# Two buffers for the merged rows, first value tiles loaded in the fronts, accumulators loaded late, normalisation in two operations

## The reference

```python
merged = sigmoid(gate_a) * (attn @ w_br_attn) + sigmoid(gate_b) * (rwkv_out @ w_br_rwkv)
h = layer_norm(ALPHA * x + merged @ w_out, ln1_g, ln1_b)
y = layer_norm(ALPHA * h + peer(h, peer_q, peer_keys, peer_u, peer_v), ln2_g, ln2_b)

def one_block(xb):                       # peer, for 128 rows
    q = (xb @ peer_q).reshape(128, 8, 2, 64)
    s = einsum("bhcd,hckd->bhck", q, peer_keys)          # 8 heads, 2 halves, 128 keys
    sv, si = top_k(s, 16)
    cand = sv[:, :, 0, :, None] + sv[:, :, 1, None, :]   # 256 candidates a head
    fv, fi = top_k(cand, 16)                             # 16 experts a head, of 16384
    gate = softmax(fv)
    act = gelu(einsum("bhkd,bd->bhk", peer_u[eidx], xb))
    return einsum("bhk,bhkd->bd", gate * act, peer_v[eidx])
```

## Time and profile before

| | us |
|---|---|
| median of 3 runs | 4496.24 (4477.59 to 4502.65) |
| the profiled execution | 4525.03 |
| its span | 4523.2 |
| early front | about 685 to 829 |
| late front | about 2547 to 3056 |
| dense stage | about 3056 to 4523 |

### The profile page before, as it was taken

How to read it: one execution, slowest core, us unless ns; L and a number is a source line. 1 busy time by engine, 2 the same in 40 slices (tenths; PEclk the granted TensorE clock), 3 DMA queues, 4 the chain that set the end, 5 groups by cost and what they waited for, 6 DMA issues and landing times. The chain is left out here.

```text
span 4523.2 us, 71734 instructions
## 1 busy us (share of the span) xinstructions
PE 3806.4 (84%) x28122; PEld 2543.4 (56%) x28122; DVE 3106.4 (69%) x6050; ACT 874.0 (19%) x1788; POOL 1830.6 (40%) x1489
## 2 busy tenths in 40 slices
PE   7977888899979688887877786667999999999997
PEld 6766665655545487876654364553544445444543
DVE  0455422578778567775967478885889888967778
ACT  1332220110222122322531012560000000000000
POOL 0016000056212133332336207834666666666774
PEclk9988888899999898987878887678999999999998
DMA  7552443399889657675559633439999999999997
GB/s 171 168 154 89 134 153 129 119 341 410 197 202 214 186 193 254 218 237 174 174 202 404 260 136 47 94 105 353 407 403 395 394 403 407 389 401 407 404 400 281
DMA packets 438548, 1154.59 MB, mean 255 GB/s; under 512 B 84497, under 2 KB 179260, under 8 KB 434588
## 3 DMA queue, kind: packets, MB, share of 16 engines
q0 software_dynamic: 207216, 687.87, 43.3%
q1 hardware_dynamic: 194564, 422.08, 27.1%
q10 hardware_dynamic: 36432, 40.05, 2.6%
HBM read 1045.72 MB, written 114.70 MB: 257 GB/s over the span
## 5 line engine op out<-in xcount | busy, mean ns | idle before, releaser
L2677 PE MATMUL x_sps<-c_big,l_c_wo 128*128 128x384 f32 x2048 | 691.8, 501 | 93.3 <-DMA l_c_wo<-u_cols 82.9
L381 POOL DMA_INDIRECT l_w_ring<-u_rows,k_eidx x256 | 300.8, 1175 | 973.7 <-DVE l_w_dots L437 443.8
L2684 PE MATMUL x_vps<-x_v,x_w 128*128 128x512 f32 x1536 | 662.3, 592 | 2.1 <-DVE x_w L2717 2.1
L381 POOL DMA_INDIRECT w_ring<-u_rows,k_eidx x384 | 482.7, 1257 | 442.9 <-DVE w_dots L437 276.3
L2677 PEld LDWEIGHTS x_sps<-c_big,l_c_wo 128*128 128x128 f32 x2048 | 400.4, 196 | 385.1 <-DMA l_c_wo<-u_cols 90.4
L454 DVE SCALAR_TENSOR_TENSOR w_yacc<-w_ring,w_wts,w_yacc 128x1024 f32<-128x1024 f32 x384 | 493.4, 1285 | 64.4 <-DMA w_ring<-v_rows,k_eidx 52.9
L2684 PEld LDWEIGHTS x_vps<-x_v,x_w 128*128 128x128 f32 x1536 | 291.7, 190 | 366.7 <-issue 357.8
L437 DVE CUSTOM_DVE_ANT_0 w_ring<-w_ring,w_h 128x1024 f32<-128x1024 f32 x384 | 452.2, 1223 | 55.2 <-DMA w_ring<-u_rows,k_eidx 28.3
L381 POOL DMA_INDIRECT w_ring<-v_rows,k_eidx x384 | 429.8, 1119 | 133.3 <-issue 113.4
L381 POOL DMA_INDIRECT l_w_ring<-v_rows,k_eidx x256 | 283.6, 1108 | 345.5 <-DVE l_w_yacc L454 283.6
L454 DVE SCALAR_TENSOR_TENSOR l_w_yacc<-l_w_ring,l_w_wts,l_w_yacc 128x1024 f32<-128x1024 f32 x256 | 329.0, 1285 | 51.4 <-DMA l_w_ring<-v_rows,k_eidx 43.0
(11 more groups left out here) (643 smaller groups left out, 6171.0 us busy)
## 6 DMA issues: line engine op xcount, KB each, us to landing
l_c_wo<-u_cols SPq DMA_DIRECT2D x128, 512.0 KB, 7.2
x_v<-v_rows SPq DMA_DIRECT2D x128, 512.0 KB, 12.2
e_c_w<-w_tiles SPq DMA_DIRECT2D x54, 512.0 KB, 3.7
l_c_w<-w_tiles SPq DMA_DIRECT2D x54, 512.0 KB, 7.4
l_c_wo<-s_G SPq DMA_DIRECT2D x16, 1536.0 KB, 23.1
s_rw<-l_q_out SPq DMA_DIRECT2D x48, 384.0 KB, 12.9
s_G<-l_f_stage ACTq DMA_DIRECT2D x8, 2048.0 KB, 8.0
s_zT<-l_pz ACTq DMA_DIRECT2D x30, 384.0 KB
```

Of the source, the lines that this page charges most:

```text
L381: pool.indirect_dma_start(out=self.ring[:, r, :], out_offset=None, in_=self.A[table], in_offset=bass.IndirectOffsetOnAxis(ap=idx[:, s:s + ...
L2677: mm = pe.matmul(sps[n % 2][:, 0:ND * P], u[n % 4][:, k, :], hT[:, k, :], start=(k == 0), stop=(k == KT - 1))
L2684: mm = pe.matmul(vps[k][:, x * 512:(x + 1) * 512], w[:, e, k * P:(k + 1) * P], v[:, e, x * 512:(x + 1) * 512], start=(c == 0 and e == 0), ...
```

## The change

- `fronts` has two buffers `mTb` with a semaphore each. `load(0)` and `load(1)` come first on SP, ahead of the decode rows' small loads, `iota`, `ln`, `wq` and `keys`; `load(i)` waits for `mix(i - 2)`.
- `wq` has no tile of its own: it lies in a tile `sb_v` of the same size, allocated around the front. In the late part this tile outlives the front and is the dense stage's v. Behind the last query of the front SP loads the first chunk's v tiles into it (`last_q`, `v_ahead`), and the front's end waits for them.
- The dense stage doesn't load v for chunk 0, and loads `acc` behind `load_v` of chunk 14 (at c = 13).
- ACT's order for i = 2: the copies of the scores come before `soften(0)`.
- In `norm`, `scaled` and `token_scaled`, (x - mean) * rs, times ln gain, plus ln offset (three operations) become ((x - mean) * gain) and (times rs + offset): two `scalar_tensor_tensor`.

```diff
-        lnk(V.tensor_scalar(x, x, ag[:, 0:1], rs, ALU.subtract, ALU.mult))
-        lnk(V.tensor_tensor(x, x, self.ln[0:rows, 0, :], ALU.mult))
-        self.mark(dve, V.tensor_tensor(x, x, self.ln[0:rows, 1, :], ALU.add), done_s, n)
+        lnk(V.scalar_tensor_tensor(x, x, ag[:, 0:1], self.ln[0:rows, 0, :], ALU.subtract, ALU.mult))
+        self.mark(dve, V.scalar_tensor_tensor(x, x, rs, self.ln[0:rows, 1, :], ALU.mult, ALU.add), done_s, n)
...
-        wq = sb("f_wq", [P, KT, DM])
+        wq = A["sb_v"]
...
-        mTb = sb("f_mTb", [P, KT, P])
+        mTb = [sb(f"f_mTb{j}", [P, KT, P]) for j in range(2)]
...
-                if i:
-                    sp.wait_ge(S["mixed"], i)
+                if i >= 2:
+                    sp.wait_ge(S["mixed"], i - 1)
...
+            load(0)
+            load(1)
             if dec_rows:
...
-            load(0)
...
-            load(1)
             n_ahead = ahead(sp, S["ahead_in"])
...
             n_ahead += last(sp, S["ahead_in"])
+            sp.wait_ge(S["q_psum"], NF)
+            n_ahead += last_q(sp, S["ahead_in"])
...
                 query(i)
+                for c in range(2):
+                    scores(i, c)
                 if picks and i == 2:
                     soften(0)
-                for c in range(2):
-                    scores(i, c)
...
             load_g(0)
             rows.begin(sp)
-            load_v(0)
-            for k, b in enumerate(DENSE):
-                sp.dma_start(acc[:, k, :], A["h"][b]).then_inc(S["acc_in"], 16)
...
                 if c + 1 < NCH:
                     load_v(c + 1)
+                if c == NCH - 3:
+                    for k, b in enumerate(DENSE):
+                        sp.dma_start(acc[:, k, :], A["h"][b]).then_inc(S["acc_in"], 16)
...
-                        pe.wait_ge(v_in[e], 16 * (c + 1))
+                        if c:
+                            pe.wait_ge(v_in[e], 16 * c)
...
+    def v_ahead(sp, sem):
+        for e in range(CH):
+            sp.dma_start(A["sb_v"][:, e, :], A["v_rows"][e * NKEY:(e + 1) * NKEY]).then_inc(sem, 16)
+        return CH
```

More of the change, by code:

```diff
@@ L2059, in finish, with fronts @@
         do(dve, "b3", V.tensor_tensor(to, to, self.gate[:, :, :], ALU.mult))
-def fronts(nc, A, tag, blocks, picks, strewn, scat, ahead, last, few=False, dec_rows=False):
+def fronts(nc, A, tag, blocks, picks, strewn, scat, ahead, last, last_q, few=False, dec_rows=False):
     NF, NST, NSC, NPK = len(blocks), len(strewn), len(scat), len(picks)
@@ L2104, in fronts @@
         gps = [psum(f"f_gps{j}", 512) for j in range(2)]
-        names = ("const_in iota_in ln_in m_in mixed h0_done var_done std_done h_done hT_psum hT_done q_psum q_done sc_psum "
+        m_in = [sem(f"f_m_in{j}") for j in range(2)]
+        names = ("const_in iota_in ln_in mixed h0_done var_done std_done h_done hT_psum hT_done q_psum q_done sc_psum "
                  "sc_done sc_out ahead_in sc_in scs_read fv_done fe_done idx_done idx_psum byslot_done one_done two_done g_psum g_done link "
@@ L2129, in load @@
             def load(i):
-                if i:
-                    sp.wait_ge(S["mixed"], i)
-                sp.dma_start(mTb[:, :, :], A["mT"][:, :, blocks[i] * P:(blocks[i] + 1) * P].rearrange("t p c -> p t c")).then_inc(S["m_in"], 16)
+                if i >= 2:
+                    sp.wait_ge(S["mixed"], i - 1)
+                sp.dma_start(mTb[i % 2][:, :, :], A["mT"][:, :, blocks[i] * P:(blocks[i] + 1) * P].rearrange("t p c -> p t c")).then_inc(m_in[i % 2], 16)
                 if i >= 2:
@@ L2202, in mix @@
                 if c == 0:
-                    pe.wait_ge(S["m_in"], 16 * i + 16)
+                    pe.wait_ge(m_in[i % 2], 16 * (i // 2) + 16)
                     if i:
@@ L2206, in mix @@
                 for k in range(KT):
-                    mm = pe.matmul(fps[:, c * 512:(c + 1) * 512], mTb[:, k, :], wo[:, k, c * 512:(c + 1) * 512],
+                    mm = pe.matmul(fps[:, c * 512:(c + 1) * 512], mTb[i % 2][:, k, :], wo[:, k, c * 512:(c + 1) * 512],
                                    start=(k == 0), stop=(k == KT - 1))
@@ L2451, in norm @@
                 lnk(V.reciprocal(rs[:, :], rs[:, :]))
-                lnk(V.tensor_scalar(hi[:, :], hi[:, :], ag[:, 0:1], rs[:, 0:1], ALU.subtract, ALU.mult))
                 if i == 0:
                     dve.wait_ge(S["ln_in"], 16)
-                lnk(V.tensor_tensor(hi[:, :], hi[:, :], ln[:, 0, :], ALU.mult))
-                mark(V.tensor_tensor(hi[:, :], hi[:, :], ln[:, 1, :], ALU.add), S["h_done"], i + 1)
+                lnk(V.scalar_tensor_tensor(hi[:, :], hi[:, :], ag[:, 0:1], ln[:, 0, :], ALU.subtract, ALU.mult))
+                mark(V.scalar_tensor_tensor(hi[:, :], hi[:, :], rs[:, 0:1], ln[:, 1, :], ALU.mult, ALU.add), S["h_done"], i + 1)
             def choose(k, x):
@@ L2531, in token_scaled @@
                 lnk(V.reciprocal(d_rs[0:NS, :], d_rs[0:NS, :]))
-                lnk(V.tensor_scalar(d_y, d_y, d_ag[0:NS, 0:1], d_rs[0:NS, :], ALU.subtract, ALU.mult))
-                lnk(V.tensor_tensor(d_y, d_y, d_ln[:, 0, :], ALU.mult))
-                mark(V.tensor_tensor(d_y, d_y, d_ln[:, 1, :], ALU.add), S["d_done"], 1)
+                lnk(V.scalar_tensor_tensor(d_y, d_y, d_ag[0:NS, 0:1], d_ln[:, 0, :], ALU.subtract, ALU.mult))
+                mark(V.scalar_tensor_tensor(d_y, d_y, d_rs[0:NS, :], d_ln[:, 1, :], ALU.mult, ALU.add), S["d_done"], 1)
             norm(0)
@@ L2599, in experts @@
         u = A["sb_u"]
-        v = sb("x_v", [P, CH, DM])
+        v = A["sb_v"]
         w = sb("x_w", [P, CH, ND * P])
@@ L2627, in load_v @@
             def load_v(c):
-                if c:
-                    sp.wait_ge(S["v_psum"], ND * c)
+                sp.wait_ge(S["v_psum"], ND * c)
                 for e in range(CH):
@@ L2792, in program @@
             trunk(PARTS[0], none, nothing, c4)
-            fronts(nc, A, "e_", [NB] + EARLY, [], [], [], x_ahead, none_ahead, few=True)
+            A["sb_v"] = c4.enter_context(nc.sbuf_tensor("e_c_v", [P, CH, DM], F32))
+            fronts(nc, A, "e_", [NB] + EARLY, [], [], [], x_ahead, none_ahead, none_ahead, few=True)
         with ExitStack() as c4:
@@ L2799, in program @@
             A["sb_hT"] = wide(ND * P)
+            A["sb_v"] = c4.enter_context(nc.sbuf_tensor("l_c_v", [P, CH, DM], F32))
+            assert CH == KT
             A["sb_u"] = [A["sb_wo"][:, j, :].rearrange("p (k n) -> p k n", k=KT) for j in range(4)]
-            fronts(nc, A, "l_", [b for b in range(NB) if b not in EARLY], DENSE + FETCHED_2[:1], STREWN, [b for b in DENSE if b not in STREWN], none_ahead, u_ahead, dec_rows=True)
+            fronts(nc, A, "l_", [b for b in range(NB) if b not in EARLY], DENSE + FETCHED_2[:1], STREWN, [b for b in DENSE if b not in STREWN], none_ahead, u_ahead, v_ahead, dec_rows=True)
             experts(nc, A)
```

## The result

| us | before | changed |
|---|---|---|
| median of 7 runs each, side by side | 4486.56 (4475.94 to 4502.65) | 4439.06 (4429.24 to 4456.68) |
| the profiled execution | 4525.03 | 4429.24 |
| its span | 4523.2 | 4427.4 |

The ratio is 0.9897, with a 95% interval from 0.9877 to 0.9916: 1.0% faster, 46.2 us of 4486.56, with an interval from 37.7 to 55.2 us (the two medians are 47.5 apart). The forecast was 4448, a ratio of 0.9893 and 48.3 us. The interval is wide: the forecast's 48.3 and the 39.7 of the rival "the fronts give less" both lie in it, and the 37.3 of "only the bytes count" is just outside. Which of them holds has to come from the stages.

What follows compares the result with a forecast made beforehand. PE's matmuls, u loads, and DVE with the gathers were taken to share the dense stage, the fronts not living on transfers. Terms -5.2, -13.8, -1.4, -3.5, -25.6, +4, -2.8 sum to -48.3: ratio 0.9893, 4448.3 us; range 4427 to 4478.

Steps and rivals of the forecast that it cites:

- the fronts give less: Rival, both fronts: the clock falls in the 1.5 us gap too (5.6) and wq is late (3); -39.7, 4457; chance 0.12.
- only the bytes count: Rival, dense stage: it gains only v's 4.2 MB, 10.6 us instead of 25.6 - 4; total -37.3, 4459; chance 0.2.
- ACT's order: Late front, i = 2: decode sums come earlier, so DVE's 1.36 us wait for them goes; -1.4 us.
- dense: chunk 0: Stall for the fifth u tile falls from 29.88 to 7 us (bounds 0 and 15); chunk 92.1 instead of 117.7, -25.6.
- acc +4: Chunk 14: acc's three loads, 1.6 MB, stand ahead of its fifth u tile; +4 us, from 0 to +8.
- Mixes and clock: Both fronts: gap before the second mix falls to 1.5 us, and the mix takes 14.00; early -5.2, late -13.8.
- the margin of 2 us: Late front: wq in before about 2581, wanted by PE at 2583.4; its later load costs nothing, or up to 3 us.
- Normalisation: Two operations for three, -0.7 us each: five on the late front's path (3.5), four at the end (2.8).
- v in the front: End of the late front: chunk 0's v lands by about 3030 to 3035, before the last store at 3047.05; cost 0.
- The mean of the others should stay at 88.1: Dense stage: chunks other than the first keep their mean of 88.1 us; a rise would mean bytes or lost lead.
- DVE loses its lead: Rival, dense stage: without the long stall gathers and v compete, 92.4 us a chunk; in all +12, 4508; chance 0.06.
- order: Dense stage: PE's chunk 0 stall comes from loads queued ahead of the fifth u tile; reordering wins it, 25.6 less 4.

Runs made afterwards that it cites:

- f1: The kernel before with only the two `mTb` buffers and the new order of the fronts' first loads; 4521.68 us, ratio 0.9954 to the kernel before.
- g2: The changed kernel with each front's second mix waiting for the first block's whole normalisation; fronts 144.0 and 490.2 us, against 137.6 and 485.4.
- n0: The changed kernel with the three-operation normalisation put back in all three places; 4503.22 us, one run.
- a1: The changed kernel with acc loaded behind the last u tile of chunk 15; 4486.64 us, ratio 0.9898 to the kernel before, dense stage 1439.3 us.
- a3: The same kernel as a1, run again beside the changed kernel on one chip; 4436.66 us, ratio 0.9894 to the kernel before, dense stage 1442.7 us.
- d1: The kernel before with chunk 0's v issued behind its u tiles and acc at c = 13, no byte leaving the stage; 4530.51 us, ratio 0.9987.

## Why the prediction was right, point by point

| us | forecast | by the stages |
|---|---|---|
| early front | -5.2 | -6.3 |
| late front: mixes, ACT's order, norms | -18.7 | -18.5 |
| dense: chunk 0 | -25.6 | -30.1 |
| dense: from chunk 1 to the end (acc +4, norms -2.8) | +1.2 | +9.3 |
| sum | -48.3 | -45.6 |

The chunk 0 row is the mean of 117.7 and 116.0 (f1) against 86.8, the mean of the five traces; the row under it 1350.7 against 1360.0.

*Mixes and clock.* Both steps came as written: gap 1.4 for 1.5, 13.97 for 14.0. That the 2.8 of the clock hangs on PE's idling is seen in g2, where it partly returned, and in the granted clock; its size at a given gap is not what I assumed (below). The row that the 14.00 was taken from was a favourable one: in the kernel before, the next two mixes of the late front took 16.71 and 16.54 without idling directly ahead of them. PE's wait ahead of the first transposes is 0.32, for the keys: wq and keys came just in time, so the margin of 2 us was used up but the term of 0 held. POOL's gathers start 5.5 us behind the first mix instead of 2.5 ahead of it and were covered. DVE's first choice in the kernel before, then DVE and POOL of the changed kernel:

```profile
2639.14 0.29 DVE L165 MAX8 k_sv<-k_scs 128x8 f32<-128x128 f32 x1 [14.27 <-DMA k_scs<-s_sc]
```

```profile
2567.54 0.29 DVE L165 MAX8 k_sv<-k_scs 128x8 f32<-128x128 f32 x1 [14.20 <-DMA k_scs<-s_sc]
...
2664.67 1.27 DVE L2520 SCALAR_TENSOR_TENSOR c_big<-c_big,l_f_gps 8x512 f32<-8x512 f32 x2
```

```profile
2500.20 0.93 POOL L2308 DMA_INDIRECT l_f_stage<-u_rows,k_didx  x1 [41.36 <-DMA k_dgate<-s_d_gate]
```

The choice comes 72.88 us behind the first mix (2567.54 less 2494.66) instead of 86.63 (2639.14 less 2552.51 in the earlier trace rows): 13.75 sooner, for 13.8. That it fits to 0.05 is partly luck. PE's part, to the end of the first block's scores, is 72.5 before and 60.8 changed, 11.7 sooner: the first mix (16.53 for 15.40) and the query (17.43 for 16.19) took longer. The other 2.1 are the scores' store and fetch, 12.0 for 14.1, which the forecast had not counted.

*ACT's order.* The decode sums at 2664.67 have no wait any more (1.36 in the earlier trace rows); undone, a wait of 2.17 was back and the front behind the first choice was 1.6 longer, for 1.4. One run.

*Normalisation.* -2.8 for -3.5 in the front (one run of n0) and -2.6 for -2.8 at the end (the same in every trace), together 5.4 for 6.3.

*v in the front.* Cost 0, as said. From ACT's last store to the first `x_sps` it is 9.34 us in both kernels (2970.68 to 2980.02; 3047.05 to 3056.39 in the earlier trace rows), though the eight loads were issued from 2937.51 on. ACT and SP of the changed kernel:

```profile
2970.68 0.37 ACTq L2382 DMA_DIRECT2D s_G<-l_f_stage  x1
```

```profile
2935.71 1.76 SPq L2753 DMA_DIRECT2D l_c_wo<-u_cols  x4
2937.51 5.05 SPq L2758 DMA_DIRECT2D l_c_v<-v_rows  x8
```

*Chunk 0, mis-sized.* The stall left over was put at 7 us, with bounds 0 and 15; it was 1.96. Half of the rate for SP beside the gathers was nearly right: by it the fifth tile comes 26.4 us after the stage's start, and it came after 25.0, which by the forecast's own working is a stall of 2.1. What failed is the step from the 3.5 us of that working to "7 us for this stall and the slower start after it, like the longest of the other chunks": no slower start followed.

*The rest of the stage, the step that failed.* "The mean of the others should stay at 88.1" did not hold. From chunk 1 to the end the stage is 9.3 longer. Of this a1 and a3 show 5.4 to be acc (1354.6 against 1360.0; forecast 4), and the norms take off 2.6, so 6.5 is left that the forecast had at 0. Chunk 1 alone is 9.6 longer. It is the mechanism of the rival that DVE loses its lead, at its place but in one chunk instead of fourteen. (That rival's "worst" chunk, 92.4, was not the worst: chunk 9 of the kernel before took 93.1, by which its sum would have been +22 instead of +12.) POOL at the start of chunk 1, first the kernel before and then the changed one, and DVE of the changed one:

```profile
3173.56 0.94 POOL L381 DMA_INDIRECT w_ring<-u_rows,k_eidx  x1 [0.30 <-issue]
3187.63 1.14 POOL L381 DMA_INDIRECT w_ring<-u_rows,k_eidx  x1 [13.13 <-DVE w_dots L437]
```

```profile
3071.62 0.93 POOL L381 DMA_INDIRECT w_ring<-u_rows,k_eidx  x1 [0.30 <-issue]
3080.56 1.14 POOL L381 DMA_INDIRECT w_ring<-u_rows,k_eidx  x1 [8.01 <-DVE w_dots L437]
```

```profile
3072.99 0.56 DVE L2717 TENSOR_TENSOR x_w<-x_w,l_c_wo 128x384 f32<-128x384 f32 x1 [1.89 <-ACT x_w L2694]
```

The first 20 us of chunk 1 as windows (columns as above), of the kernel before and of the changed one:

```profile
3174.07:3194.07 20.00, 20.00 (x64) 11.78 (x63) 9.40 (x14) 1.57 (x4) 5.67 (x5) 1.00 1.03 410
```

```profile
3067.00:3087.00 20.00, 20.00 (x63) 11.78 (x62) 13.29 (x24) 1.57 (x4) 9.58 (x9) 1.00 1.03 410
```

Before, the ring was full and POOL stood still for 13.13 us; with five gathers in these 20 us, more of the same 410 GB/s was SP's. Changed, the pause is 8.01, POOL has nine gathers in these 20 us, DVE's idle time falls from 7.01 to 1.89, and the fifth u tile comes 6.71 late. Later chunks alternate between 82 to 85 and about 91 to 92 as they did before. The place is read from the traces, and d1 (91.8 in chunk 1) shows that removing the stall alone brings it about.

How far the gathers were ahead can be counted: gathers that POOL has started, less the tiles that DVE has begun to multiply or add. At the start of chunk 1 it is 10, all the buffers, in the two traces with the long stall (before and f1: chunk 1 82.5), and 7 or 8 in the twelve others (87.7 to 92.8). The same holds further on. In chunks 1 to 13 of all fourteen traces, the 25 chunks that started with 10 tiles ahead took 82.5 to 84.9, mean 83.3; the 78 that started with 7 or fewer had a mean of 91.0 and none was below 84.8; 8 and 9 lie between (89.0 and 85.4). So the lead goes with the chunk's length wherever one looks, and one or two long chunks rebuild it (in the changed kernel it was 7, 10, 7 at chunks 1, 2, 3, which took 92.4, 82.6 and 92.4). It remains an association: no run set the lead by itself.

*Between "order" and "bytes".* The rival "only the bytes count" said 4459 and the forecast 4448: in reductions 37.3 and 48.3, with 46.2 by the timing. The sum was right, what it was credited to was not. In d1, with the order but not the bytes, the stage gave 4.6 of the 21.6 that the forecast had for order alone (25.6 less 4). The changed kernel's dense stage is 16.2 shorter than d1's (1463.0 less 1446.8); the norms are 2.6 of that, so 13.6 are left for the 4.2 MB of v that leave the stage, 10.6 at the full rate. Nearly all of it lies in chunk 0 (98.6 against 86.8), where in d1 DVE stood for gathered rows while v was on the way; from chunk 1 on d1 took 1364.3 and the changed kernel, with the norms put back, 1362.6. Of the 20.8 of the stage, the bytes are thus the larger part (13.6) and the order the smaller (4.6). This is a difference between one trace and the mean of five. The Trainium skill's statement (DMA: Bandwidth & Descriptors, Issuing engines are not separate DMA queues) that transfers of all issuing engines run on the same 16 engines and interleave agrees with d1, where DVE waited 6.75 us for rows that POOL had asked for while SP's loads of v ran.

So the total was right in part by luck, with two errors that partly cancel: 4.5 too little for chunk 0 (and 1.1 for the early front), and 8.1 too much credit behind it.

## What to carry to other kernels

Where the DMA engines are full, a long stall of the matmul engine is no measure of what removing it gives: ask first which bytes leave the stage, and look at the chunk behind the stall for what the stall had been giving to others. Loads moved into a stage whose engines have room (v in the front) gained their whole transfer here (13.6 us for 4.2 MB), and a load that nobody awaits (acc) belongs behind the last one that somebody does. Compare traces by the stage that is touched, and for a small term by a stretch between two of its own events: untouched stages here varied by more than the whole effect, the late front by 3 us, and the stretch from the last gathered add to the end by less than 0.1.

## What the hardware showed that I had not expected

- After an idle gap PE's 32 matmuls took 13.97 us (gap 1.4), 16.75 (3.88), 15.48 (6.44) and 16.82 (12.47). The price is not monotonic in the gap; it is half of the time that the mix spent at the half clock, 0, 5.6, 3.0 and 5.6 us. When the clock falls and returns is set by more than the gap before the mix, and no run varied it.
- The late trunk took 1675 to 1756 us from trace to trace with nearly the same code, and the kernel before took 4486 in two of the comparisons and 4543 to 4545 in two others. The two go together by chip: 1735 to 1756 in the eight traces from the two chips with 4543 to 4545, 1683 to 1695 in the four from the chip with 4486. The first traces of the kernel before and of the changed one, for which no chip is on record, have 1720 and 1675.
- In the dense stage 18.9 MB more cost 2.1 us a megabyte, and 4.2 MB fewer, taken from a chunk that was near its floor already (82.5 us of PE's own work, 84 with DVE's waits), gave nothing clear of the spread.
- A chunk's length went with how many gathered tiles were ahead when it started: 83.3 us on average with all ten buffers, 91.0 with seven or fewer.
